# Differential attention: the combination of the two softmax maps split by columns between VectorE and GpSimd

## The reference

```python
s = jnp.einsum('bqhid,bkhid->bhiqk', q, k, preferred_element_type=jnp.float32) * (DA ** -0.5)
p = jax.nn.softmax(s, axis=-1)
w = p[:, :, 0] - lam * p[:, :, 1]
return jnp.einsum('bhqk,bkhd->bqhd', w.astype(v.dtype), v)
```

## Time and profile before

| what | value |
|---|---|
| median of 3 runs | 3975.33 us (3975.26 to 3977.81) |
| profiled execution, its time | 3972.31 us |
| span of that execution | 3970.2 us |
| instructions | 53080 |
| granted clock of PE over the span | 0.993 of 2.4 GHz |
| GpSimd busy | 319.7 us, 8% |

### The profile page before, as it was taken

The page is one execution under the profiler, slowest core; times in us unless marked ns, Lnnn a source line. Parts: engine busy times, 40 slices in busy tenths (PEclk is TensorE's granted clock), DMA queues, the critical chain, the costliest instruction groups (busy, mean ns, idle before and its releaser), DMA issues. The chain is left out here.

```text
span 3970.2 us, 53080 instructions
## 1 busy us (share of the span) xinstructions
PE 3839.5 (97%) x20276; PEld 3030.8 (76%) x20276; DVE 2232.9 (56%) x3890; ACT 1540.6 (39%) x2617; POOL 319.7 (8%) x282
## 2 busy tenths in 40 slices
PE   7999999999999999999999999999899999999998
PEld 5876567778888888875788788876578887667887
DVE  5355678754553543365734556276657626666752
ACT  3245661113431322255722344253544415354431
POOL 0100001111000001100000100114010010400001
PEclk9999999999999999999999999999999999999999
DMA  5210015551221121200022233322023323202332
GB/s 192 84 38 26 1 52 184 200 180 58 64 69 56 63 73 57 70 25 26 17 95 79 85 97 100 100 92 80 19 89 98 96 91 98 75 28 89 95 103 82
DMA packets 81206, 320.10 MB, mean 81 GB/s; under 512 B 9728, under 2 KB 9856, under 8 KB 80128
## 3 DMA queue, kind: packets, MB, share of 16 engines
q1 hardware_dynamic: 68064, 270.49, 21.0%
q0 software_dynamic: 12960, 47.19, 3.5%
HBM read 311.09 MB, written 2.10 MB: 79 GB/s over the span
## 5 line engine op out<-in xcount | busy, mean ns | idle before, releaser
L529 DVE TENSOR_TENSOR split_low<-weight_ring,split_high 128x1024 fp32r<-128x1024 f32 (+2 forms) x408 | 555.2, 1361 | 510.3 <-ACT split_high L521 510.1
L521 ACT ACTIVATE split_high<-weight_ring 128x1024 fp32r<-128x1024 f32 (+2 forms) x412 | 466.4, 1133 | 871.5 <-PE banks L1587 338.7
L1787 PE MATMUL banks<-normed_high,split_high 128*128 128x512 f32 x1040 | 405.6, 390 | 3.0 <-DVE normed_low L1730 2.2
L1787 PE MATMUL banks<-normed_low,split_high 128*128 128x512 f32 x1040 | 404.7, 389 | 0.0
L1787 PE MATMUL banks<-normed_high,split_low 128*128 128x512 f32 x1040 | 404.7, 389 | 0.0
L2085 PE MATMUL banks<-normed_high,split_high 128*128 128x512 f32 (+1 forms) x704 | 238.7, 339 | 2.1 <-DVE normed_low L2000 2.1
L2085 PE MATMUL banks<-normed_low,split_high 128*128 128x512 f32 (+1 forms) x704 | 237.6, 337 | 0.0
L2085 PE MATMUL banks<-normed_high,split_low 128*128 128x512 f32 (+1 forms) x704 | 237.1, 337 | 0.0
L1787 PEld LDWEIGHTS banks<-normed_high,split_high 128*128 128x128 f32 x1040 | 195.2, 188 | 47.3 <-DVE normed_low L1730 3.0
L1787 PEld LDWEIGHTS banks<-normed_high,split_low 128*128 128x128 f32 x1040 | 195.2, 188 | 40.7
L1787 PEld LDWEIGHTS banks<-normed_low,split_high 128*128 128x128 f32 x1040 | 195.2, 188 | 40.0
(11 more groups left out here) (391 smaller groups left out, 8483.7 us busy)
## 6 DMA issues: line engine op xcount, KB each, us to landing
weight_ring<-in_up SPq DMA_DIRECT2D x174, 512.0 KB, 3.5
weight_ring<-in_down SPq DMA_DIRECT2D x64, 704.0 KB, 4.1
modulation_ring<-in_ada POOLq DMA_DIRECT2D x80, 512.0 KB, 4.1
weight_ring<-in_merge SPq DMA_DIRECT2D x48, 768.0 KB, 4.4
weight_ring<-in_inputs SPq DMA_DIRECT2D x36, 512.0 KB, 3.4
weight_ring<-in_out SPq DMA_DIRECT2D x32, 512.0 KB, 3.5
weight_ring<-in_xbc SPq DMA_DIRECT2D x16, 512.0 KB, 3.5
weight_ring<-in_short SPq DMA_DIRECT2D x12, 512.0 KB, 3.5
```

The costliest lines, as they stand in the source:

```text
L521: act.activation(k.splits[0][:, (n0 + panel) % RING, 0:width], k.slot(n0 + panel)[:, 0:width], ACT.Copy).then_inc(k.high_ready.sem, 1)
L529: dve.tensor_tensor(k.splits[1][:, s, 0:width], k.ring[:, s, 0:width], k.splits[0][:, s, 0:width].bitcast(F32), ALU.subtract).then_inc(k.l ...
L1787: last = pe.matmul(sums(r, half), w, x, start=(c + j == 0), stop=(c == KT - 1 and j == 2))
```

## The change

In steps of 512 keys or more of the differential attention (here those of 768) the columns are halved. VectorE combines columns 0 to 383 in its one instruction as before. GpSimd combines columns 384 to 767 in two instructions: it multiplies the second map in place by the factor, then adds it to the first map. The small product on VectorE signals inverse_ready in place of vector_link; VectorE waits for it, and so does GpSimd. Between its two instructions GpSimd waits for its own first (weighted_ready). PE waits for GpSimd's second (weighted_added) beside probs_ready before it turns a map. Steps of 256 keys stay whole on VectorE.

```diff
--- before.py
+++ after.py
@@ -1088,7 +1088,26 @@
     def result(t):
         return k.psum[:, 6 + groups[t] % 2, 0:P]
 
+    pooled = [sum(combined and step["keys"] >= BANK for step in steps[:t + 1]) for t in range(U)]
+
+    def own_columns(t):
+
+        return steps[t]["keys"] if steps[t]["keys"] < BANK else steps[t]["keys"] // 2
+
     with nc.Block() as block:
+        @block.gpsimd
+        def _(pool):
+            for t in range(U if combined else 0):
+                a, b = own_columns(t), steps[t]["keys"]
+                if a == b:
+                    continue
+                first, second = probs(2 * t)[:, a:b], probs(2 * t + 1)[:, a:b]
+                pool.wait_ge(*k.inverse_ready(t + 1))
+                pool.tensor_scalar(second, second, one(inverses, 2 * t + 1), None, ALU.mult).then_inc(
+                    k.weighted_ready.sem, 1)
+                pool.wait_ge(*k.weighted_ready(pooled[t]))
+                pool.tensor_tensor(first, first, second, ALU.add).then_inc(k.weighted_added.sem, 1)
+
         @block.tensor
         def _(pe):
             def score(t):
@@ -1106,6 +1125,8 @@
             def turn(t, j):
                 n = per * t + j
                 pe.wait_ge(*k.probs_ready(n + 1))
+                if combined and pooled[t]:
+                    pe.wait_ge(*k.weighted_added(pooled[t]))
                 if n >= 1:
                     pe.wait_ge(*k.turned_copied(n))
                 for c, size in chunks(steps[t]):
@@ -1173,11 +1194,12 @@
                     dve.wait_ge(*k.output_stored(t - 2))
                 link(dve.reciprocal(inverse, total))
                 if combined and j == 1:
-                    link(dve.scalar_tensor_tensor(inverse, inverse, one(sums, m - 1), step["subtract"], ALU.mult,
-                                                  ALU.mult))
-                    first = probs(m - 1)
-                    dve.scalar_tensor_tensor(first, p, inverse, first, ALU.mult, ALU.add).then_inc(
-                        k.probs_ready.sem, 1)
+                    dve.scalar_tensor_tensor(inverse, inverse, one(sums, m - 1), step["subtract"], ALU.mult,
+                                             ALU.mult).then_inc(k.inverse_ready.sem, 1)
+                    dve.wait_ge(*k.inverse_ready(t + 1))
+                    first, width = probs(m - 1), own_columns(t)
+                    dve.scalar_tensor_tensor(first[:, 0:width], p[:, 0:width], inverse, first[:, 0:width], ALU.mult,
+                                             ALU.add).then_inc(k.probs_ready.sem, 1)
                 elif combined:
                     pass
                 elif step["gate"] is not None:
@@ -1280,7 +1302,8 @@
             for t in range(U - 2, U) if scratch is not None else ():
                 square(t)
     k.ends(scores_ready=2 * U, max_ready=2 * U, exp_ready=2 * U, probs_ready=per * U, probs_turned=per * U,
-           turned_copied=per * U, output_ready=U, output_stored=sum(step["last"] for step in steps),
+           turned_copied=per * U, output_ready=U, inverse_ready=U if combined else 0,
+           weighted_ready=pooled[-1], weighted_added=pooled[-1], output_stored=sum(step["last"] for step in steps),
            vector_link=k.linked, squares_ready=0 if scratch is None else U,
            scaled_ready=0 if beside is None else 4, rounded_ready=0 if beside is None else len(beside[0]),
            normed_ready=0 if beside is None else len(beside[0]))
```

## The result

| what | before | after |
|---|---|---|
| median | 3975.3 us (4 runs, 3975.14 to 3977.81) | 4003.6 us (4 runs, 3999.55 to 4005.57) |
| profiled execution, span | 3970.2 us | 4002.4 us |
| layer 0 attention, first score to last store | 88.1 us | 98.8 us |
| layer 1 attention, first score to last store | 65.3 us | 80.5 us |
| all the rest of the span | 3816.7 us | 3823.1 us |

A forecast was written before the change was run, and what follows sets the result against it. The prediction took PE and VectorE as nearly full, with the combination's end on the path to turn and next score. Layer 1's 9.4 us and layer 0's 6.1 summed to 15.5 slower: 3990.8 us, range 3982.5 to 4001.

The forecast's parts named there:

- The loop from a score to its turn: Layer 1 rounds: maximum 1.59 us after the score, combination 4.00, turn 5.13, next score behind it; 7.27 for two rounds.
- 0.54 us off VectorE gave 0.04: Layer 0, round after a 256-column combination: 3.56 us against 3.60, so relieving VectorE alone gains at most about 2.5 us.
- The new wait: PE before the turn: waits for GpSimd's addition, turn 6.33 us after the score instead of 5.13, 1.20 late.
- The collision: GpSimd's multiplication stands still beside VectorE's combination, ending at 5.09 us after the score; undisturbed 4.73.
- point 3: GpSimd's work on 384 columns: multiplication 0.62 us, between ends of 0.45 and 1.03, and addition 1.03.
- the prediction's own signs of being wrong: Changed profile: GpSimd multiplication outside 0.45 to 1.03 us, a turn still waiting for VectorE, or clock under 0.97 in either stage.
- the same walk: Both attention stages, round by round, each instruction starting after its engine's last and its waits: 9.4 and 6.1 us slower.
- a clock under 0.97 in a stage: PE's granted clock in either attention stage of the changed profile: below 0.97 would make the prediction wrong.
- the falling clock: Rival, PE in both stages: idling lowers the granted clock to 0.94, 8 us more, 23 slower; chance 0.05.
- GpSimd is slower than the rows suggest: Rival, GpSimd's half: multiplication 1.03 us gives 22 us slower, with an addition of 1.29 26.5; chance 0.14.
- The collision is absent: Rival, multiplication beside VectorE's combination: no standstill, turn 0.84 us late, 9.4 us slower or 7.5; chance 0.17.
- Not slower: Rival, at the turn: GpSimd's work and hand-overs fit in 1.16 us from ready factor; 2.5 us faster, 3973; chance 0.03.

The follow-up runs named there:

- the cheaper multiplication: The changed kernel with GpSimd multiplying by a TENSOR_TENSOR with the factor broadcast, in place of the TENSOR_SCALAR: 3992.4 us against 3975.6, ratio 1.0044.
- one sixth: The changed kernel with VectorE combining 640 columns and GpSimd 128, multiplying by a broadcast TENSOR_TENSOR: 3979.5 us against 3974.8 for the kernel before, ratio 1.0009.

## Why the prediction was wrong

**Right: what bounds the stages.** The loop from a score to its turn and to the score two rounds on was there to the hundredth (1.59, 4.00, then the turn), and its two-round period grew by just the lateness of the turn, 9.02 for 7.27 at 1.74 us late. "0.54 us off VectorE gave 0.04" held for the whole change: with GpSimd's part left out the stages give back 1.8 and 0.4 us, forecast 2.0 and 0.5.

**Right: the mechanism.** The new wait of PE takes the place of the combination, with the weighing and the next score behind it; moving the weighing ahead took it from 28.3 to 15.8 us. The collision was there, 0.42 us where the forecast had 0.36, and by its rule: the multiplication ends its own time less 0.13 after VectorE's combination (1764.58 + 0.62 + 1.24 - 0.13 = 1766.31). The addition took 0.99 for 1.03.

**Wrong: point 3, the multiplication.** It was put at 0.62 between bounds of 0.45 and 1.03, "with one operand to read in place of two I take half the slope". Its own time is 1.24, outside both bounds, and that was one of the prediction's own signs of being wrong. The step that failed is the assumption that a TENSOR_SCALAR can't cost more than a TENSOR_TENSOR of the same columns. On this engine it costs more than the addition (0.99) and more than the same product written as a TENSOR_TENSOR (0.83). With the collision the multiplication ends at 5.73 after the score, forecast 5.09.

What that is worth: the turn is 1.74 late, forecast 1.20. Putting the measured 1.66 and 0.99 into the same walk gives 10.9 us for layer 0 and 14.1 for layer 1, 25.0, where the stages measure 26 to 28. So of the 12.8 us between forecast and result, 9.5 are this one term (the addition and the hand-overs came out slightly shorter than forecast). With it right the forecast would have been some 4000.3 us, just inside the range; it took the remainder too to carry the result past 4001.

**The remainder** against the stages is some 1 to 3 us. Two things that the walk lacks are in the profile.

The first is the clock. One half-clock stretch lies in layer 0 and two in layer 1. In the first of layer 1 a score took 2.20 us in place of 1.56 (at 1746.01), and the turn under way then 1.51 in place of 0.87. The text said that a clock under 0.97 in a stage would speak against it: it is 0.96 in layer 1 by the windows. I gave the falling clock 0.05 and 8 us, with "PE stays busier than 80%" against it; PE was busy 82% of layer 1, and the stretches came all the same, though at a far smaller size: by the two profiles of before one stretch can cost up to 1.55 us.

The second is one more collision, which I had overlooked. In layer 0 VectorE's small product, 0.22 us everywhere else in this profile, took 0.94, 0.54, 0.55 and 0.56 us, once in each head, in the round that scores the first step of 256 keys. The maxima of that round are short (0.42 us), so VectorE comes to the product of the last 768-key step while GpSimd still adds for the one before it:

```profile
262.12 0.99 POOL L1109 TENSOR_TENSOR probs_turned<-probs_turned 128x384 f32<-128x384 f32 x1
262.18 0.94 DVE L1197 SCALAR_TENSOR_TENSOR scalars<-scalars 128x1 f32<-128x1 f32 x1
...
263.16 0.62 DVE L1201 SCALAR_TENSOR_TENSOR probs<-probs,scalars 128x384 f32<-128x384 f32 x1
```

The product ends 0.01 after the addition (263.12 for 263.11), and the combination and GpSimd's multiplication, which wait for it, start late by the difference, 1.7 us over the four. The kernels with the cheaper multiplication, whose additions end earlier, have no such long product. How the remainder divides between the two is not shown, and nor is how much of the 1.7 us reaches the end of the stage. In layer 1 of the changed kernel's first profile no product is long, and it lost 15.1 with its two stretches where the walk has 14.1. With 256 columns for GpSimd neither is in the profile, and the stages lost 17.2 us against the profile of before that has no stretch either, where the walk had 17.

**The rivals.** "GpSimd is slower than the rows suggest" came true, at 22 us by its own numbers, and for a reason that it did not have, since its multiplication was 1.03 "like a two-operand one" and needed a disturbed addition to go further. The upper end of the range, 26 us, took in most of that rival and was still short, because both bounds of the multiplication were taken from another instruction. "The collision is absent" fell with the 0.42 us. "Not slower" is bounded, not tested: with one sixth of the columns the loss shrank to 4.6 us, but the turn still came 1.54 after the ready factor, past the 1.16 that the rival needed.

**The price by the Trainium skill.** The text set the Trainium skill (GPSIMD Engine Reference, Engine selection) beside the sum: one-input work roughly at line rate, an estimate of 0.32 us for these columns from its 1.2 GHz. The trace disagrees: 1.24 undisturbed. The same section's advice, to keep elementwise work on VectorE, holds: 0.62 us there against 2.23 on GpSimd (1.24 + 0.99) for the same 384 columns. Its figure of about two for work with two inputs holds as well: 1.29 us for 512 columns on GpSimd, 0.69 on VectorE.

## What to carry to other kernels

An instruction that the trace of an engine does not show has no upper bound from its neighbours; before moving work, look for the same operation in the same form, and where it is missing let the range reach well past the nearest row (here that row was 1.03 us, and the instruction took 1.24 alone and 1.66 beside VectorE). Work taken off an engine is worth only what its idle time would not have absorbed: one round with a short instruction in it, such as that of the 256-key combination, tells this before anything is built. When a piece of a value comes from a slow engine, see what is queued behind the consumer's wait, and move that ahead first. Run the new order without the slow engine too: here it gave back 12.5 us beside the wait and cost 4.9 without it. Look for collisions not only between the two halves of one step, but also between one step's slow half and the next step's small instructions.

## What the runs showed that I had not expected

- GpSimd's TENSOR_SCALAR of 128x384 f32 in place takes 1.24 us alone, the product of the same columns with a broadcast column as TENSOR_TENSOR 0.83, a TENSOR_TENSOR addition 0.99. A constant in place of the pointer gives 1.59 for 1.66, beside VectorE. In every profile with the TENSOR_SCALAR its line also has a pair of MODIFY_POOL_CONFIG at the start of the stage (243.8 us in the changed kernel, 11 ns each); with the TENSOR_TENSOR there is none. Whether the two facts belong together no run shows.
- How long the held engine stands still follows one pattern. GpSimd, held behind VectorE's two-operand instruction, lost the overlap less 0.13 or 0.14 us: 0.42 of 0.55 (TENSOR_SCALAR, 384 columns), 0.20 of 0.33 and 0.47 of 0.60 (the additions of the cheaper multiplication and of one sixth), and 0.85 of 0.99 in the earlier trace rows. VectorE, held behind GpSimd, ended about its own time less 0.2 after it: 0.40 and 0.42 us for a combination of 0.62, 0.68 for one of 0.88, 0.01 for the product of 0.22.
- Which engine stands still is not told by the recorded starts alone. With the TENSOR_SCALAR starting 0.07 us after VectorE's two-operand combination, GpSimd lost 0.42 us and VectorE nothing (0.62). With the TENSOR_TENSOR starting 0.04 to 0.05 us after it, GpSimd lost nothing and VectorE 0.66 (1.28). With GpSimd's addition 0.02 us ahead, VectorE lost 0.77 (1.39). The Trainium skill (SBUF — State Buffer, SBUF: two separate sides) says that, of GpSimd and a VectorE instruction with two inputs in SBUF, the one that starts first gets the pair of ports that they share for the whole instruction; the first and third case agree by their starts, the second does not. Either a TENSOR_TENSOR on GpSimd needs less time from its recorded start to its first read than a TENSOR_SCALAR, or the limit lies near 0.05 us for both: the TENSOR_SCALAR with a constant came 0.052 us or more after VectorE and lost, the multiplications by TENSOR_TENSOR came 0.044 after it and won. No run separates the two.
- Outside the changed stages the span moved between 3816.7 and 3824.2 us over 13 profiles, in which the code there was the same.
